# One bias product per half of an expert's hidden row, with a selector kept in memory

## The chip, the cores and the metric

The kernel runs on one core of a Trainium2 chip. A core has TensorE (PE; its weight loads are listed as PEld), VectorE (DVE), ScalarE (ACT), GpSimd (POOL), a sync engine (SP) that issues most transfers here, and 16 DMA engines that the queues share. The metric is the device time of one launch in microseconds, lower is better. Before the change: 1108.92 us, the median of 3 runs (1108.81 to 1109.72).

## The reference

One decoder layer on 256 positions of width 1024, in float32. Its first half (an mLSTM group and an attention group of heads, then an output projection) ends in a residual stream x. Then comes the part that the change touches, a mixture of experts:

```python
logits = (t @ w_router + b_router)            # t: 256 x 1024, the normed stream
top_vals, top_idx = lax.top_k(logits, TOP_K)  # 4 of 32 experts
for e in range(N_EXPERTS):                    # 32
    hu = t @ w_gu[e] + b_gu[e]                # 1024 -> 2048
    glu = jnp.minimum(hu[:, :D_FF], SWIGLU_LIMIT)
    lin = jnp.clip(hu[:, D_FF:], -SWIGLU_LIMIT, SWIGLU_LIMIT)
    act = glu * jax.nn.sigmoid(SWIGLU_ALPHA * glu) * (lin + 1.0)
    y = y + gates[:, e:e + 1] * (act @ w_dn[e] + b_dn[e])
```

After it a gate product of 1024 x 1024 with a per-layer embedding is added. An expert's weights are 12 MB, those of all experts 403 MB, and each byte is read once.

## The kernel before

**Experts.** Each expert works on up to 64 positions (SLOTS), its own, gathered out of the 256 by a product with a one-hot matrix. If some expert has more, the whole expert loop is run again over the rest; in the profiled run it goes through once. Experts are taken in pairs, 16 of them (PAIRS). The gathered rows of a pair lie transposed in `xg` (in `xg0` for the first pair): 8 blocks of 128 input rows, 128 columns, 64 for each expert of the pair.

**The hidden row.** `hu` is PSUM, 4 banks of 128 partitions x 512. Expert e of a pair uses banks 2e (the gate half, b = 0) and 2e + 1 (the linear half, b = 1). The 1024 columns of each half are folded: columns 0 to 511 (n = 0) go to partitions 0 to 63, columns 512 to 1023 (n = 1) to partitions 64 to 127. A product `mm(out, weights, moving)` loads `weights` (rows x output partitions) and streams `moving` (rows x 512) through them. Each float32 product shows as two records in the profile. `up_block` (line 1091) does this for one block of 128 input rows: four products of 64 output partitions each, for b and n. `up_chunk` (line 1137) takes one 2 MB piece of weights, two such blocks; an expert has four of these, then two 2 MB pieces for `down_chunk` (line 1158).

**The bias.** `bias` (line 126) is a tile of 128 rows x 1024. Rows 0 to 31 hold columns 0 to 1023 of `b_gate_up` for the 32 experts, rows 32 to 63 hold columns 1024 to 2047, rows 64 to 95 hold `b_down`. Two DMAs of 128 KB fill the first two (lines 488 and 489), behind SP's wait for `gate_step` and before the loads of `negbc` and `w_out`. `up_bias` (line 1084) adds an expert's row to `hu` by four products, for b and n: the weights are one column of an identity (`sel_part`, rows 32b to 32b + 31), repeated 64 times by a stride of zero, so that every output partition receives the row of that expert.

**Order on PE.** The order is written out by hand. In a pair: the chunks of expert 0 with the scatter of the pair before in between; the first chunk of expert 1; the transposes of expert 0's activation (`act_transposes`, line 1100); the bias of expert 1 (line 1211); expert 0's down products; the rest of expert 1; the gather for the next pair (`gather_half`, line 1039, one-hot products); transposes of expert 1; the bias of the next pair's expert 0 (line 1253); expert 1's down products. The bias of the very first expert stands behind its third chunk (line 1156). Down products wait for ACT's copy of the transposed activation (line 2001).

**The ring of weights.** Eleven slots of 2 MB. SP issues the loads in order of use (`load_position`, line 496; line 514 is nearly every one of them), each when PE has finished with the slot's previous content (`chunk_done`). The last two loads into it are those of the final gate product (line 599).

**DVE and ACT in the loop.** `activation(e)` (line 1668) on DVE takes the minimum and clip of `hu`, ACT's `sigmoid` (line 1995) writes into the same bank, DVE multiplies. Then PE transposes and ACT copies (`transposed_act`, line 1999).

**Memory that the change uses.** `num_xg` holds early things and then, in the loop, expert output (columns 0 to 511), the one-hot matrix (512 to 767), and `gatesT` on partitions 64 to 95 of columns 768 to 1023. Partitions 0 to 63 of these columns are free in the loop. `ident` is a 128 x 128 identity.

Of the kernel before, what the change touches and what calls it, by code (L numbers as in the profile page):

```python
# [33 lines left out]
def hybrid_layer(nc, x, p, mix_norm_g, w_in, conv_w, conv_b, igate_b, fgate_b, mlstm_head_g, q_norm_g,  # L34
# [66 lines left out]
    with ctx:  # L101
# [94 lines left out]

        xg = num_xg[:, VX:VX + K * P].rearrange("p (k s) -> p k s", k=K)
        onehot = num_xg[:, NB:NB + S].rearrange("p (t e s) -> p t e s", t=TT, e=2)
        gatesT = num_xg[64:64 + E, NB + S:NB + 2 * S]
        ghot = early[:, 0:2 * S].rearrange("p (t e r s) -> p t e r s", t=TT, e=2, r=2)  # L200
        ghotT = early[:, 2 * S:4 * S].rearrange("p (e t) -> p e t", e=2)
# [127 lines left out]
        ghotT_ready = sem("ghotT_ready")  # L329
        xg_ps = sem("xg_ps")  # L330
        xg_ready = sem("xg_ready")
        glu_ready = sem("glu_ready")
        lin_ready = sem("lin_ready")
        sig_ready = sem("sig_ready")
# [14 lines left out]
        w_pp_k = w_ple_proj[0].rearrange("(k p) n -> p k n", p=P)  # L349
        gu_src = w_gate_up[0].rearrange("e (p c k) n -> e c p (k n)", c=4, k=2)  # L350
        dn_src = w_down[0].rearrange("e (h p f) n -> e h p (f n)", h=2, f=4)
        x_src = x[0].rearrange("(t p) d -> p t d", p=P)
        p_src = p[0, 0].rearrange("(t p) d -> p t d", p=P)
        out_dst = out[0].rearrange("(t p) d -> p t d", p=P)
# [106 lines left out]
        def _(sp):  # L461
# [23 lines left out]
            load(CHUNK_WO_B, slot(CHUNK_WO_B, D, 4), w_out_k[:, 4:8, :])  # L485
            sp.wait_ge(gate_step, GATE_STEPS)
            sp.dma_start(w_r[:], w_router[0].rearrange("(k p) e -> p k e", p=P)).then_inc(wr_loaded, 16)
            for j in range(2):
                sp.dma_start(bias[32 * j:32 * j + E, :], b_gate_up[0][:, j * D:(j + 1) * D]).then_inc(late_loaded, 16)
            sp.dma_start(bias[64:64 + E, :], b_down[0]).then_inc(late_loaded, 16)  # L490
            sp.wait_ge(negm_stored, 16)
            sp.dma_start(negbc.rearrange("p h s -> p (h s)"), negm_d.rearrange("h s -> (h s)").rearrange("(o n) -> o n", o=1)
# [202 lines left out]
        def _(pe):  # L695
# [381 lines left out]
                              start=(k == 0), stop=(k == PLE // P - 1))  # L1077
                last.then_inc(ple_ps, 1)

            def expert_rows(part, expert):  # L1080

                return sel_part[32 * part:32 * part + E, expert:expert + 1].to_broadcast([E, SLOTS])

            def up_bias(e, expert, first):

                for b in range(2):
                    for n in range(HALVES):
                        mm(hu[n * SLOTS:(n + 1) * SLOTS, 2 * e + b, :], expert_rows(b, expert),  # L1088
                           bias[32 * b:32 * b + E, n * NB:(n + 1) * NB], start=first, stop=False, skip_group_check=True)

            def up_block(e, rows_of, w, k, first, halves=range(2)):

# [39 lines left out]
            with pe.Fori(0, npass) as ps:  # L1132
                for pair in range(PAIRS):
# [3 lines left out]
                    def up_chunk(e, c):  # L1137
                        m = position(pair, 0, e, c)
                        if m in HALVED:
                            wait_half(pe, ps, m)  # L1140
                        wait_position(pe, ps, m)
                        if m == RING + 1:
                            pe.wait_ge(next_half, ps * 16 + 16)
                        w = moe_slot(m)
                        rows_of = xg if pair else xg0
                        first = c == 0 and (e == 1 or pair == 0)
                        if m == 0:
                            for b in range(2):
                                up_block(e, rows_of, w, 0, first, [b]).then_inc(half_done, 1)
                        else:  # L1150
                            last = up_block(e, rows_of, w, 2 * c, first)
                        if m == 1:
                            last.then_inc(half_done, 1)
                        up_block(e, rows_of, w, 2 * c + 1, False).then_inc(chunk_done, 1)
                        if c == 2 and e == 0 and pair == 0:
                            up_bias(0, 0, False)

                    def down_chunk(e, h, bank):
# [49 lines left out]
                        pe.wait_ge(ghotT_ready, pairs + (pair + 1))  # L1208
                    pe.wait_ge(act_ready, experts + (2 * pair + 1))
                    act_transposes(2 * pair)  # L1210
                    up_bias(1, 2 * pair + 1, False)
                    if pair == 0:
                        pe.wait_ge(gates_ready, TT)
                        gate_rows()
                    if pair < PAIRS - 1:
                        if pair == PLE_PAIR:
                            wait_position(pe, ps, PLE_AT)
                            pe.wait_ge(y_done, ps * (QUADS * ROUNDS) + (pair * QUADS + QUADS))
                            embedding_transposes()
                        pe.wait_ge(actT_ready, experts + (2 * pair + 1))  # L1220
                        down_chunk(0, 0, po[:, 0, :])
                        if pair == PLE_PAIR:
                            pe.wait_ge(pT_ready, ps + 1)
                            ple_quad(0)
                        down_chunk(0, 1, po[:, 0, :])
                        if pair == PLE_PAIR:
                            ple_quad(1)
                        if pair == NEXT_PAIR:
                            pe.wait_ge(onehot_ready, pairs + (selections(pair) + 1))
                            pe.wait_ge(y_done, ps * (QUADS * ROUNDS) + (pair * QUADS + QUADS))  # L1230
                            for c in range(2):
                                gather_half(c, aux[:, c, :])
                        up_chunk(1, 1)
                        if pair == PLE_PAIR:
                            ple_quad(2)
                        up_chunk(1, 2)
                        if pair == PLE_PAIR:
                            ple_quad(3)
                        up_chunk(1, 3)

                        pe.wait_ge(onehot_ready, pairs + (selections(pair) + 2))
                        if pair == PLE_PAIR:
                            pe.wait_ge(ple_ready, ps * QUADS + QUADS)
                        elif pair == NEXT_PAIR:
                            pe.wait_ge(xg_ready, ps * (2 * PAIRS) + (gathers(pair) + 2))
                        elif pair == 0:
                            pe.wait_ge(gatesT_ready, ps + 1)
                        pe.wait_ge(y_done, ps * (QUADS * ROUNDS) + (pair * QUADS + QUADS))
                        for c in range(2):
                            gather_half(c, aux[:, c, :])  # L1250
                        pe.wait_ge(act_ready, experts + (2 * pair + 2))
                        act_transposes(2 * pair + 1)
                        up_bias(0, 2 * pair + 2, True)
                        pe.wait_ge(out_s_ready, experts + (2 * pair + 1))
                        pe.wait_ge(actT_ready, experts + (2 * pair + 2))
                        for h in range(2):
                            down_chunk(1, h, po[:, 0, :])
                        if pair == 0:
                            pe.wait_ge(ghot_ready, pairs + 1)
                            ghot_transposes()  # L1260
                    else:
                        for c in range(1, 4):
                            up_chunk(1, c)
                        pe.wait_ge(actT_ready, experts + (2 * pair + 1))
                        down_chunk(0, 0, po[:, 0, :])
                        pe.wait_ge(act_ready, experts + (2 * pair + 2))
                        act_transposes(2 * pair + 1)
                        down_chunk(0, 1, po[:, 0, :])
                        pe.wait_ge(actT_ready, experts + (2 * pair + 2))
                        w = moe_slot(POSITIONS - 2)  # L1270
                        pe.wait_ge(down_half, ps * 16 + 16)
                        down_rows(2 * pair + 1, 0, w, hu[:, 0, :], range(0, 2))
                        pe.wait_ge(out_s_ready, experts + (2 * pair + 1))
                        pe.wait_ge(y_done, ps * (QUADS * ROUNDS) + (pair * QUADS + QUADS))
                        for q in range(HALVES):
                            scatter_expert(q, 0, LAST_BANKS[q])
                        wait_position(pe, ps, POSITIONS - 2)
                        down_rows(2 * pair + 1, 0, w, hu[:, 0, :], range(2, 4)).then_inc(chunk_done, 1)
                        down_chunk(1, 1, hu[:, 0, :])
# [489 lines left out]
        def _(act):  # L1769
# [214 lines left out]
            for tt in range(TT):  # L1984
                act.wait_ge(negtop_ready, tt + 1)
                a.activation(gates[:, tt, :], lg[:, tt, :], ACT.Exp, bias=stat[:, 32 + tt:33 + tt]).then_inc(route_exp, 1)

            act.wait_ge(npass_ready, 1)
            npass = act.value_load(npass_i[0:1, 0:1], min_val=1, max_val=S // SLOTS)
            with act.Fori(0, npass) as ps:  # L1990
                for pair in range(PAIRS):
# [3 lines left out]
                    def sigmoid(e):  # L1995
                        act.wait_ge(glu_ready, experts + (2 * pair + e + 1))
                        a.activation(hu[:, 2 * e, :], gated(2 * pair + e), ACT.Sigmoid, scale=ALPHA).then_inc(sig_ready, 1)  # L1997

                    def transposed_act(e):
                        act.wait_ge(actT_ps, experts + (2 * pair + e + 1))  # L2000
# [92 lines left out]
```

## Time and profile before

| what | value |
|---|---|
| median of 3 runs | 1108.92 us |
| profiled execution | 1109.2 us |
| its span | 1107.0 us |
| granted clock of TensorE, mean | 0.998 of full speed |
| PE busy | 1069.9 us, 97% of the span |
| DVE, ACT, POOL busy | 258.4, 144.7, 17.3 us |
| moved by DMA | 431.89 MB, 390 GB/s over the span |
| bias products (line 1088) | 256 records, 34.8 us busy |

The span is the time from the first to the last instruction that the profile has; some microseconds lie around it. Busy time of PE counts the records' union, in which each record is a few tenths of a microsecond longer than the step to the next one, since matmuls are pipelined. How long a group really occupies PE is read from the starts of the pieces in the chain of waits, where the next piece begins when the last is through.

### The profile page before, as it was taken

To read this page: it belongs to the slowest core of one execution; us is meant where nothing else is said; L and a number is where in the kernel's file an instruction comes from. 1 tells how busy PE (TensorE), PEld (TensorE's weight loads), DVE (VectorE), ACT (ScalarE), POOL (GpSimd) and SP (SyncE) were. 2 spreads that over 40 slices of the span, in tenths; PEclk is the share of its full clock that TensorE was granted. 3 is DMA by queue.
4 is the path that set the end of the run, shared out by engine and by line. 5 is a ranking of instruction groups with operands and counts; after the bars stand their busy time and mean duration, and the time that the engine had idled before them with its cause. 6 is when DMAs were issued, how large, how long until landed. Compare 5 with 4: busy or idle time off the path is not lost.

```text
span 1107.0 us, 12035 instructions
## 1 busy us (share of the span) xinstructions
PE 1069.9 (97%) x5130; PEld 445.0 (40%) x5130; DVE 258.4 (23%) x531; ACT 144.7 (13%) x283; POOL 17.3 (2%) x45
## 2 busy tenths in 40 slices
PE   9999999999999999999999899998989999999898
PEld 5485563434343434343434232333333344433234
DVE  4274241231121212121212121111212021212122
ACT  4134341100000000000000000000000100000022
POOL 2001100000000000000000000000000000000000
PEclk9999999999999999999999999999999999999999
DMA  9943589999999999999999999999999999999981
GB/s 348 368 163 123 242 350 384 427 428 427 427 427 429 427 427 426 429 428 427 427 429 429 427 426 429 429 428 426 427 428 426 427 428 428 427 428 427 425 342 38
DMA packets 43004, 431.89 MB, mean 390 GB/s; under 512 B 6231, under 2 KB 6751, under 8 KB 17606
## 3 DMA queue, kind: packets, MB, share of 16 engines
q1 hardware_dynamic: 42736, 431.07, 93.1%
q8 instruction: 41, 0.67, 0.2%
q14 instruction: 13, 0.11, 0.0%
q10 hardware_dynamic: 214, 0.04, 0.0%
HBM read 430.04 MB, written 1.06 MB: 389 GB/s over the span
## 4 chain that ended last, share of the span: by engine, by line
PE 69%; DMA 30%; DVE 0%; issue 0%; ACT 0%; ACTq 0%; DVEq 0%
PE hu L1096 23%; DMA ring<-in_w_gate_up 22%; PE po L1126 15%; DMA ring<-in_w_down 8%; PE aux L1043 5%; PE hu L723 5%; PE hu L729 3%; PE aux L1051 3%; PE hu L739 2%; PE hu L1088 2%; PE hu L765 1%; PE aux L1303 1%; PE po L1103 1%; PE aux L1076 1%; PE hu L1126 1%; PE po L1303 1%
## 5 line engine op out<-in xcount | busy, mean ns | idle before, releaser
L1096 PE MATMUL hu<-ring,num_xg 128*64 128x512 f32 x1920 | 431.6, 596 | 24.1 <-DMA ring<-in_w_gate_up 24.1
L1096 PEld LDWEIGHTS hu<-ring,num_xg 128*64 128x64 f32 x1920 | 131.5, 137 | 304.2 <-issue 257.2
L1126 PE MATMUL po<-ring,arena 128*64 128x512 f32 x976 | 219.3, 600 | 7.2 <-DMA ring<-in_w_down 7.2
L1126 PEld LDWEIGHTS po<-ring,arena 128*64 128x64 f32 x976 | 67.9, 137 | 154.3 <-issue 139.9
L1674 DVE TENSOR_SCALAR arena<-hu 128x512 f32<-128x512 f32 x31 | 21.4, 692 | 432.0 <-PE hu L1096 432.0
L1650 DVE TENSOR_TENSOR arena<-arena,aux 128x512 f32<-128x512 f32 x58 | 37.3, 684 | 133.3 <-PE aux L1051 121.4
L1043 PEld LDWEIGHTS aux<-num_xg,big 128*128 128x128 f32 x512 | 58.4, 192 | 13.0 <-issue 13.0
L1043 PE MATMUL aux<-num_xg,big 128*128 128x128 f32 x512 | 61.4, 278 | 0.0
L723 PE MATMUL hu<-ring 128*128 128x512 f32 x128 | 56.7, 595 | 0.0
L1997 ACT ACTIVATE hu<-arena 128x512 f32<-128x512 f32 x31 | 18.6, 601 | 249.0 <-DVE arena L1674 249.0
L1663 DVE TENSOR_SCALAR arena<-iota_s,posm,gates 128x128 f32<-128x128 f32 x64 | 17.9, 342 | 118.2 <-PE po L1126 115.3
L2013 ACT COPY arena<-po 128x512 f32<-128x512 f32 x16 | 9.4, 586 | 220.6 <-PE po L1116 220.6
L1051 PE MATMUL aux<-num_xg,arena 64*128 64x512 f32 x124 | 35.0, 641 | 0.1
L723 PEld LDWEIGHTS hu<-ring 128*128 128x128 f32 x128 | 23.8, 190 | 27.7 <-issue 27.4
L1088 PE MATMUL hu<-bias,sel_part 32*64 32x512 f32 x256 | 34.8, 612 | 0.0
L1051 PE MATMUL aux<-arena 64*128 64x512 f32 x124 | 31.8, 589 | 0.0
L2001 ACT COPY arena<-po 128x512 f32<-128x512 f32 x31 | 18.2, 586 | 90.3 <-PE po L1103 90.3
L729 PE MATMUL hu<-ring 128*128 128x256 f32 x128 | 29.5, 385 | 0.0
L1096 PE MATMUL hu<-ring,arena 128*64 128x512 f32 x128 | 28.1, 594 | 0.1
L729 PEld LDWEIGHTS hu<-ring 128*128 128x128 f32 x128 | 23.7, 190 | 4.8 <-DVE ring L1453 1.0
L739 PE MATMUL hu<-ring 128*128 128x512 f32 (+1 forms) x64 | 25.5, 541 | 0.0
L2005 ACT COPY num_xg<-po 128x512 f32<-128x512 f32 x16 | 9.4, 586 | 114.9 <-PE po L1126 114.9
(275 smaller groups left out, 606.5 us busy)
## 6 DMA issues: line engine op xcount, KB each, us to landing
ring<-in_w_gate_up SPq DMA_DIRECT2D x125, 2048.0 KB, 36.0
ring<-in_w_down SPq DMA_DIRECT2D x60, 2048.0 KB, 36.1
ring<-in_w_in SPq DMA_DIRECT2D x6, 2048.0 KB, 16.2
ring<-in_w_gate_up SPq DMA_DIRECT2D x6, 1024.0 KB, 7.7
ring<-in_w_out SPq DMA_DIRECT2D x2, 2048.0 KB, 12.2
ring<-in_w_down SPq DMA_DIRECT2D x4, 1024.0 KB, 37.6
ring<-in_w_ple_gate SPq DMA_DIRECT2D x2, 2048.0 KB, 34.1
ring<-in_w_in SPq DMA_DIRECT2D x4, 512.0 KB, 6.5
```

Source lines behind the costliest of these rows:

```text
L723: last = mm(bank, hT[:, k, tt * P:(tt + 1) * P], slot(n, NB, K)[:, k, :], start=(k == 0), stop=(k == K - 1))
L729: last = mm(bank[:, 0:S], slot(n, NB, K)[:, k, ct * P:(ct + 1) * P], hT[:, k, :], start=(k == 0), stop=(k == K - 1))
L739: last = mm(bank[:, lo:hi], mixT[:, k, tt * P:(tt + 1) * P], slot(n, D, 4)[:, k % 4, b * NB + lo:b * NB + hi], start=(k == 4), stop=(k == 3))
L1043: last = mm(bank[:, (k % 4) * P:(k % 4 + 1) * P], h2[:, tt, k * P:(k + 1) * P], onehot[:, tt, :, :].rearrange("p e s -> p (e s)"), start=( ...
L1051: return mm(bank, ghotT[r, e, tt * P:(tt + 1) * P], out_s[e][r, :], start=(e == 0), stop=(e == 1 and not more))
L1088: mm(hu[n * SLOTS:(n + 1) * SLOTS, 2 * e + b, :], expert_rows(b, expert), bias[32 * b:32 * b + E, n * NB:(n + 1) * NB], start=first, stop= ...
L1096: last = mm(hu[n * SLOTS:(n + 1) * SLOTS, 2 * e + b, :], rows_of[:, k, e * SLOTS:(e + 1) * SLOTS], w[:, o:o + NB], start=first, stop=(k == ...
L1126: last = mm(bank[n * SLOTS:(n + 1) * SLOTS, :], actT[:, f, h * SLOTS:(h + 1) * SLOTS], w[:, o:o + NB], start=(h == 0 and f == 0), stop=(h ...
L1303: last = mm(fin_bank(q, lo, hi), x3T[:, k, tt * P:(tt + 1) * P], final_slot(k // 4, D, 4)[:, k % 4, n * NB + lo:n * NB + hi], start=(k == ...
L1650: v.tensor_tensor(quad(xt, q), quad(xt, q), banks[q], ALU.add).then_inc(y_done, 1)
L1674: v.tensor_scalar(glu, hu[:, 2 * e, :], LIMIT, None, ALU.min).then_inc(glu_ready, 1)
L1997: a.activation(hu[:, 2 * e, :], gated(2 * pair + e), ACT.Sigmoid, scale=ALPHA).then_inc(sig_ready, 1)
```

## The change

The bias rows are loaded in another layout: rows 32n to 32n + 31 hold column half n, both the gate part and the linear part, 64 rows in all. `up_bias` then needs one product for b instead of two: 64 rows by 128 output columns. Its weights are no longer a repeated column but a real tile, `bias_rows`, of 64 rows x 128: for an expert x, row x is one in the left 64 columns, and row 32 + x is one in the right 64. ACT writes it by one copy for each expert (`selector`), out of `ident` with a repeated column, alternating between two places. The first two are written before the loop, after the first gather, the one for expert x + 2 right behind the sigmoid of expert x. PE waits for a new semaphore, `bias_rows_ready`, before each `up_bias`.

```diff
+        bias_rows = num_xg[0:HALVES * E, NB + S:NB + 2 * S].rearrange("p (i n s) -> p i n s", i=2, n=HALVES)
...
+        bias_src = b_gate_up[0].rearrange("e (b n c) -> n e b c", b=2, n=HALVES)
...
-            for j in range(2):
-                sp.dma_start(bias[32 * j:32 * j + E, :], b_gate_up[0][:, j * D:(j + 1) * D]).then_inc(late_loaded, 16)
+            for n in range(HALVES):
+                sp.dma_start(bias[E * n:E * n + E, :].rearrange("e (b c) -> e b c", b=2), bias_src[n]).then_inc(late_loaded, 16)
...
-            def expert_rows(part, expert):
-
-                return sel_part[32 * part:32 * part + E, expert:expert + 1].to_broadcast([E, SLOTS])
-
             def up_bias(e, expert, first):
 
                 for b in range(2):
-                    for n in range(HALVES):
-                        mm(hu[n * SLOTS:(n + 1) * SLOTS, 2 * e + b, :], expert_rows(b, expert),
-                           bias[32 * b:32 * b + E, n * NB:(n + 1) * NB], start=first, stop=False, skip_group_check=True)
+                    mm(hu[:, 2 * e + b, :], bias_rows[:, expert % 2, :, :].rearrange("p n s -> p (n s)"),
+                       bias[0:HALVES * E, b * NB:(b + 1) * NB], start=first, stop=False, skip_group_check=True)
...
+                            pe.wait_ge(bias_rows_ready, experts + 1)
                             up_bias(0, 0, False)
...
+                    pe.wait_ge(bias_rows_ready, experts + (2 * pair + 2))
                     up_bias(1, 2 * pair + 1, False)
...
+                        pe.wait_ge(bias_rows_ready, experts + (2 * pair + 3))
                         up_bias(0, 2 * pair + 2, True)
...
+            def selector(expert):
+
+                both = ident[0:HALVES * E, 0:HALVES * E].rearrange("p (n e) -> p n e", n=HALVES)
+                a.copy(bias_rows[:, expert % 2, :, :], both[:, :, expert:expert + 1].to_broadcast([HALVES * E, HALVES, SLOTS]))\
+                 .then_inc(bias_rows_ready, 1)
+
+            act.wait_ge(xg_ps, 2)
+            selector(0)
+            selector(1)
...
                         a.activation(hu[:, 2 * e, :], gated(2 * pair + e), ACT.Sigmoid, scale=ALPHA).then_inc(sig_ready, 1)
+                        selector((2 * pair + e + 2) % E)
```

## Rows read from the trace of the kernel before

**Rows 1.** strips by slice, the whole span.
```profile
PE   9999999999999999999999899998989999999898
DMA  9943589999999999999999999999999999999981
GB/s 348 368 163 123 242 350 384 427 428 427 427 427 429 427 427 426 429 428 427 427 429 429 427 426 429 429 428 426 427 428 426 427 428 428 427 428 427 425 342 38
```

**Rows 2.** stretches; at the end of a row clock, DMA share, GB/s.
```profile
120.00:140.00 20.00, 20.00 (x89) 12.01 (x88) 5.46 (x12) 4.21 (x11) 2.31 (x2) 1.00 0.79 326
176.00:200.00 24.00, 24.00 (x121) 7.91 (x118) 2.68 (x4) 2.14 (x4) 0.00 (x0) 1.00 1.01 430
1080.00:1100.00 20.00, 20.00 (x63) 10.92 (x62) 5.83 (x14) 7.17 (x14) 0.00 (x0) 1.00 0.10 40
```

**Rows 3.** groups on PE; busy us, mean ns, idle before, releaser.
```profile
L1096 PE MATMUL hu<-ring,num_xg 128*64 128x512 f32 x1920 | 431.6, 596 | 24.1 <-DMA ring<-in_w_gate_up 24.1
L1126 PE MATMUL po<-ring,arena 128*64 128x512 f32 x976 | 219.3, 600 | 7.2 <-DMA ring<-in_w_down 7.2
L1088 PE MATMUL hu<-bias,sel_part 32*64 32x512 f32 x256 | 34.8, 612 | 0.0
L1060 PE MATMUL aux<-bias,num_xg 32*128 32x512 f32 x8 | 4.0, 613 | 0.0
```

**Rows 4.** chain of waits: start us, us, what, xrecords; four pieces.
```profile
177.72 1.02 PE hu L1088 x8
437.19 1.91 PE aux L1060 x4
511.71 1.02 PE hu L1088 x8
542.37 40.04 DMA ring<-in_w_gate_up
```

**Rows 5.** line 514, all expert weight loads; us from issue to landing.
```profile
DMA to landing us min/median/max: 7.1/36.0/46.7
```

**Rows 6.** line 514, the one load issued at 182.4 us.
```profile
DMA to landing us min/median/max: 11.6/11.6/11.6
```

**Rows 7.** line 514, the one load issued at 233.0 us.
```profile
DMA to landing us min/median/max: 10.2/10.2/10.2
```

**Rows 8.** weight loads of lines 1088 and 1060; ns min/median/max.
```profile
L1088 PEld LDWEIGHTS hu<-bias,sel_part x256: 127/129/131, 177.6 to 1038.7; 32*64 32x64 f32 x128
L1060 PEld LDWEIGHTS aux<-bias,num_xg x8: 181/184/185, 437.1 to 445.5; 32*128 32x128 f32 x8
```

**Rows 9.** timeline of PE, first and last of 28 waits for weights.
```profile
577.55 3.65 PE L1096 MATMUL hu<-ring,num_xg 128*64 128x512 f32 x16 [1.04 <-DMA ring<-in_w_gate_up]
1058.89 3.65 PE L1126 MATMUL po<-ring,arena 128*64 128x512 f32 x16 [0.47 <-DMA ring<-in_w_down]
```

**Rows 10.** PE's waits from 822 us to the end: us, times, longest.
```profile
PE hu L1096 <- DMA ring<-in_w_gate_up: 5.2, 6, 1.2
PE po L1126 <- DMA ring<-in_w_down: 3.4, 3, 1.6
```

**Rows 11.** line 1887, the nearest ACT copy to the selector.
```profile
L1887 ACT COPY num_xg<-aux x8: 268/268/271, 114.7 to 140.0; 128x130 f32<-128x130 f32 x8
```

**Rows 12.** timeline of ACT around one bias group: start us, us.
```profile
508.38 0.60 ACT L1997 ACTIVATE hu<-arena 128x512 f32<-128x512 f32 x1 [3.73 <-DVE arena L1674]
511.75 0.59 ACT L2001 COPY arena<-po 128x512 f32<-128x512 f32 x1 [2.77 <-PE po L1103]
```

**Rows 13.** timeline of SP's queue: start us, us, issue.
```profile
41.72 7.83 SPq L489 DMA_DIRECT2D bias<-in_b_gate_up  x2
53.99 0.39 SPq L468 DMA_DIRECT2D ring<-in_w_out  x1
```

**Rows 14.** last loads (line 599); what held line 1303.
```profile
DMA to landing us min/median/max: 31.9/34.1/36.4
  DMA ring<-in_w_ple_gate: 0.2, 1
```

More of the change, by code:

```diff
@@ L331, in hybrid_layer @@
         xg_ready = sem("xg_ready")
+        bias_rows_ready = sem("bias_rows_ready")
         glu_ready = sem("glu_ready")
```

## The prediction

> **What bounds the kernel now.** I read four views, in this order. First the strips by slice: PE is busy everywhere, but from the eighth slice to the thirty-eighth the DMA strip is at 9 and the rate stands at 425 to 429 GB/s [rows 1]. Two things are full at once, and only one can set the end. Then the table of stretches: the DMA share is 0.79 at 120 to 140 us, 1.01 at 176 to 200 us, and 0.10 at 1080 to 1100 us [rows 2]. So the run has three parts: up to about 176 us PE works through the layer's first half and the DMA engines have gaps; from there to about 1074 us they never stop; after that PE alone works off the last products. Then the groups: in the middle PE idles 24.1 us for gate/up weights and 7.2 us for down weights, 31.3 us in all, and hardly for anything else [rows 3]. That is 31.3 us in which PE had nothing to multiply. Last the chain of waits and the time from issue to landing: the chain runs along PE until 542 us, then crosses to a weight load that took 40 us to land [rows 4]. A 2 MB load that goes out alone lands in 7.1 us; the one issued at 182.4 us took 11.6, the one at 233.0 us 10.2, the median 36.0 and the longest 46.7 [rows 5 to 7]. At about 428 GB/s 2 MB move in 4.9 us, so those 36 us are a queue. PE frees slots faster than the DMA engines refill them, the queue grows, and from 577 us on PE waits for it. The chain follows single releases and so credits PE until 542 us; a load that is issued later behind a queue of several others lands no later. My reading: the expert loop is bound by the weight stream, and PE's work counts only before 176 us, after 1074 us, or where it grows beyond its own waits.
>
> **The change part by part.**
> *The products.* Before, an expert's bias costs four products: part b of two, column half n of two. Each is two records, 8 per expert, 256 in all. The four use different rows (0 to 31, 32 to 63) and different output columns (0 to 63, 64 to 127), and the trace shows them side by side: 8 records pass in 1.02 us of the chain [rows 4], 0.13 us per record, where line 1060 needs 0.48. After the change there are two products on the same 64 rows, each over all 128 output columns, so the second can't run beside the first. The trace has no 64-row one of this kind alone, but line 1060 is near: 32 rows, 128 columns, two products on the same rows. Its 4 records take 1.91 us [rows 4]. I read this as a first weight load that shows, 0.18 us [rows 8], and 4 records of (1.91 - 0.18) / 4 = 0.43 us. The old group has the same form: 0.13 us [rows 8] and two steps of 0.43 us are 0.99 of its 1.02. So the new group costs 1.91 us, and the old one 1.02: 0.89 us more for each expert, over 32 experts 28.5 us more of PE. Halving the number of products makes the work longer. If the weight load is hidden, it is 1.72 us, 0.70 more, 22.4 in all. If each of the 4 records shows its own weight load, it is 4 x (0.43 + 0.18) = 2.44 us, 1.42 more, 45.4 in all. Should a product of this kind cost no more than half of the present group, PE would save 0.51 us per expert, the bound on the other side. I take 0.89, by line 1060.
>
> The Trainium skill, "TensorEngine Tiling (Array Packing)", Theoretical Speedup, says that products with at most 64 contraction rows and at most 64 output columns can share the array, up to twice in each direction. It speaks against this change: the old form used the sharing in both directions (the trace agrees: 8 records in 1.02 us), the new one gives both up. By that rule taken strictly, with an array shared four ways, the old group would be 0.86 us and the new one 1.72; that is 0.86 more and 27.5 in all, and the end comes out as with my value.
>
> *What hides it.* PE's waits for weights are the cover: 31.3 us against 28.5 [rows 3]. The order matters, since a lag can only be paid off by a later wait. The first wait is at 577.55 us, the last at 1058.89 [rows 9], 28 in number. Walking through them with 0.89 added at each bias group: PE is 14.2 us behind at 577 us (16 groups), pays this back in the waits up to 820 us, is on time at 820 us, is up to 2.6 us behind in the heavier pairs 12 to 15, and on time again at 1054 us. From 822 us on there are 8.6 us of waits [rows 10] and 8 groups at 0.89, 7.1 us, so 1.5 us remain. Net at the end: 0. The price at which this cover is gone is 31.3 / 32 = 0.98 us per expert.
>
> *What is late next.* A lag of PE also frees slots later. That costs only where the DMA queue is short. The shortest is the load issued at 233.0 us, with 10.2 us to landing [rows 7]; three bias groups come before it, 2.7 us, which leaves 7.5 against 7.1 for a lone load [rows 5]. The one at 182.4 us has 11.6 and one group ahead of it: 10.7 left [rows 6]. So at 233 us the stream is just unbroken; with a start a little slower it would lose 0.1 to 0.3 us. I put down +0.1 us. Later the queue outgrows the lag: near 577 us it is some 46 us long against 14.2.
>
> *The selector on ACT.* 34 copies of 64 x 128. The nearest row is a 128 x 130 copy, 0.27 us [rows 11]; bounds 0.1 and 0.6 (a 512-wide one, [rows 12]). In the loop it stands between the sigmoid, which ends at 508.98 us, and the copy that starts at 511.75 us when PE has transposed [rows 12]: 2.7 us free, 0.27 used, and 2.1 still free if it were 0.6. Behind it on ACT only that copy waits, and DVE's release by the sigmoid stands before it. The first two selectors run after the first gather, near 168 us; PE wants the first at 177.72 [rows 4], and ACT's next work, the first sigmoid, comes after the chunk behind that. Cost 0.
>
> *PE's added waits.* The selector for an expert is written one whole expert earlier, so the wait is met when it is reached. Behind it are the down products of the previous expert. Nothing on PE stands still; a passed wait already sits before the transposes and shows no gap. Cost 0, and if each took 0.1 us, the price per expert would be 0.99, on the threshold.
>
> *The bias loads.* The same 256 KB in pieces of 2 KB instead of 4 KB. SP is occupied by them for 7.83 us from 41.72 us; then it has two small issues, the last done at 50.5 us, and its next work is at 53.99 us, when PE frees a slot [rows 13]. Free in between: 3.5 us. If the issue took twice as long, the w_out load would go out 4.3 us later, at 58 us, but PE reads it after 135 us; the gate/up load at 71.6 us waits for PE anyway. Cost 0.
>
> *The tail.* The last gate product starts when the first of its two loads lands: its weight load waited 0.2 us for it [rows 14]. From there PE works alone for 28 us. No bias is in there.
>
> **Sum.** Span 1107.0 + 0.1 = 1107.1; the profiled execution took 1109.2, 2.2 more than its span, so it would take 1109.3. The median of the runs is 1108.92, 0.3 under the profiled one. I forecast 1109.1 us: no change that can be measured.
>
> **The rivals.**
> *PE becomes the bound (slower).* One mechanism: the new group costs over 0.98 us more than the old one, because weight loads show inside it. If two of its four records show theirs: 1.72 + 2 x 0.18 = 2.08, 1.06 more, 33.9 in all, less 31.3: +2.6, 1111.7 us. If all four do: 45.4 - 31.3 = +14.1, 1123.3 us. For it: the cover left is only 2.8 us over the whole loop. Against it: line 1060 has the same pattern on the same rows and shows one load, not four. Its sign would be that no PE wait for weights is left. Chance 0.16.
> *The chain is right (slower).* If PE's stretch up to 542 us counts as the chain has it [rows 4], the 15 groups in it add 13.3 us: 1122.4. Against it: a DMA share of 1.01 from 176 us, and landing times that only grow. Chance 0.03.
> *The merged product is cheaper.* At half of the old group PE saves 16 us, and all of it turns into more waiting for weights: 1108.9 us. The time is the same as in my forecast. Chance 0.06.
> *Something in the stream gets faster,* for instance because fewer loads are queued. The rate is 430 GB/s at 176 to 200 us with a short queue [rows 2] and mostly 427 or 428 later; if the whole loop ran at 430, 0.5% of some 900 us, 4.5 us, 1104.8. Against it: it is 425 to 429 in every later slice, whether loads take 12 or 46 us. Chance 0.07.
> *The cover holds, nothing moves,* my forecast: 0.68.
>
> **How the numbers follow.** A difference of 0.2%, 2.2 us, is about what can be told from none here. Same: forecast 0.68 and cheaper product 0.06, less 0.02 for spread: 0.72. Slower: 0.16 and 0.03, plus 0.01: 0.20. Faster: 0.08 with spread. The range goes down to 1106.8, which leaves 0.07 below it, and up to 1113.5, which takes in the case of two shown weight loads and leaves about 0.1 for the larger ones.
>
> **What would show it.** The bias group should have 128 records on PE, and pieces of 1.9 us in place of 1.02 (wrong if under 1.1 or over 2.1). PE's waits for weights should shrink from 31.3 us to about 3 and begin near 815 us rather than 577; the DMA strip should stay full and its rate 428 GB/s; landing times should be shorter in the middle (about 32 us at 577 us rather than 46) and as before at the end. The forecast is wrong if no PE wait remains before the last down products, or if the DMA share has a hole near 235 us of more than some tenths.

## The result, and the profile after

The changed kernel takes 1111.37 us (median of 22 runs, 1110.62 to 1113.79), the kernel before in the same session 1109.34 us (22 runs, 1108.06 to 1111.52): a ratio of 1.0019, 95% interval [1.0013, 1.0025]. It is slower by 2.0 us. That is just inside the 0.2% that the forecast called no change, but the interval leaves out 1: with this many runs it is a real loss, and small as it is, its cause can be pointed at. The profiled execution took 1111.1 us, its span is 1108.9.

The strips of the changed kernel, busy tenths and GB/s:

```profile
PE   9999999999999999999999999998989999999998
DMA  9943589999999999999999999999999999999981
GB/s 349 365 163 126 244 350 389 414 393 428 428 427 428 428 426 428 428 427 427 428 428 427 427 428 427 427 428 427 428 427 426 426 430 428 426 428 427 426 352 39
```

The DMA strip reads as before, 9 after 9, and hides the loss. The rate shows it: the eighth and ninth slices, 194 to 249 us, have 414 and 393 GB/s where [rows 1] have 427 and 428. The table of stretches finds the holes. A row has the length of the stretch, the busy time of PE, PEld, DVE, ACT and POOL with their records, and at its end TensorE's clock, the DMA share and GB/s:

```profile
176.00:200.00 24.00, 24.00 (x104) 8.26 (x102) 2.67 (x4) 2.35 (x5) 0.00 (x0) 1.00 1.01 429
214.00:244.00 30.00, 29.93 (x139) 10.26 (x136) 12.17 (x21) 2.69 (x6) 0.00 (x0) 1.00 0.97 384
220.00:222.00 2.00, 2.00 (x12) 0.90 (x12) 1.13 (x5) 1.16 (x2) 0.00 (x0) 1.00 0.79 246
226.00:228.00 2.00, 2.00 (x10) 0.63 (x10) 1.54 (x3) 0.00 (x0) 0.00 (x0) 1.00 0.93 287
232.00:234.00 2.00, 2.00 (x10) 0.67 (x12) 1.91 (x3) 0.00 (x0) 0.00 (x0) 1.00 0.89 254
```

The kernel before has, for the same 30 us:

```profile
214.00:244.00 30.00, 29.93 (x144) 10.22 (x142) 12.18 (x21) 2.95 (x5) 0.00 (x0) 1.00 1.01 428
```

30 us at 384 instead of 428 GB/s are 30 x 44 / 428 = 3.1 us of stream that did not flow. At 200 us nothing is missing yet, and from 260 us on nothing more is lost. The same two long stretches, first of the kernel before, then of the changed one:

```profile
176.00:260.00 84.00, 83.93 (x421) 30.92 (x417) 19.22 (x32) 6.86 (x12) 0.00 (x0) 1.00 1.01 429
260.00:1060.00 800.00, 768.72 (x3804) 288.83 (x3805) 154.04 (x276) 61.40 (x104) 0.00 (x0) 1.00 1.01 427
```

```profile
176.00:260.00 84.00, 83.93 (x388) 31.14 (x386) 18.81 (x31) 7.49 (x15) 0.00 (x0) 1.00 1.00 413
260.00:1060.00 800.00, 790.60 (x3703) 303.17 (x3700) 154.37 (x276) 67.00 (x132) 0.00 (x0) 1.00 1.01 427
```

The groups on PE in the changed kernel (busy us, mean ns, idle before), and the weight loads of the new bias products (ns min/median/max):

```profile
L1094 PE MATMUL hu<-ring,num_xg 128*64 128x512 f32 x1920 | 429.4, 595 | 8.2 <-DMA ring<-in_w_gate_up 8.2
L1124 PE MATMUL po<-ring,arena 128*64 128x512 f32 x976 | 216.7, 595 | 1.7 <-DMA ring<-in_w_down 1.7
L1086 PE MATMUL hu<-bias,num_xg 64*128 64x512 f32 x128 | 63.4, 615 | 0.0
L1086 PEld LDWEIGHTS hu<-bias,num_xg x128: 182/187/187, 177.6 to 1042.5; 64*128 64x128 f32 x128
```

The chain of waits (start us, us, what; three pieces), answering to [rows 4]:

```profile
177.68 1.91 PE hu L1086 x4
523.27 1.91 PE hu L1086 x4
721.16 41.81 DMA ring<-in_w_gate_up
```

Half the records, and 1.91 us for a group in place of 1.02. PE's waits for weights fell from 31.3 us to 9.9, and the chain stays on PE until 721 us instead of 542. The first and the last wait that are left:

```profile
753.24 3.65 PE L1094 MATMUL hu<-ring,num_xg 128*64 128x512 f32 x16 [0.47 <-DMA ring<-in_w_gate_up]
1060.79 3.65 PE L1124 MATMUL po<-ring,arena 128*64 128x512 f32 x16 [0.47 <-DMA ring<-in_w_down]
```

The last one answers to the second of [rows 9]: the same product started at 1058.89 before and at 1060.79 now, both times when its weights landed. PE is on time; the weights are 1.9 us late. Behind it nothing differs.

On ACT the selector (the COPY with `num_xg<-ident`) takes 0.28 us and ends 2.6 us before the copy that it could delay:

```profile
519.93 0.60 ACT L2007 ACTIVATE hu<-arena 128x512 f32<-128x512 f32 x1 [3.73 <-DVE arena L1675]
520.47 0.28 ACT L1992 COPY num_xg<-ident 64x128 f32<-64x128 f32 x1
523.31 0.58 ACT L2012 COPY arena<-po 128x512 f32<-128x512 f32 x1 [2.56 <-PE po L1101]
```

### The profile page after: what moved, and what is told of

Read it like the earlier page. It is cut to its first block, busy times and chain, and to the rows that moved or that the text cites. A ratio compares the mean times of both kernels' runs of the same rounds, so it can differ in the third digit from the quotient of the medians.

```text
span 1108.9 us, 11814 instructions
## 1 busy us (share of the span) xinstructions
PE 1093.1 (99%) x5002; PEld 460.1 (41%) x5002; DVE 258.3 (23%) x531; ACT 151.9 (14%) x317; POOL 17.3 (2%) x45
## 4 chain that ended last, share of the span: by engine, by line
PE 84%; DMA 15%; DVE 0%; issue 0%; ACT 0%; ACTq 0%; DVEq 0%
PE hu L1094 32%; PE po L1124 17%; DMA ring<-in_w_gate_up 11%; PE aux L1046 5%; PE hu L726 5%; PE hu L1086 5%; PE aux L1054 4%; DMA ring<-in_w_down 3%; PE hu L732 3%; PE hu L742 2%; PE po L1101 1%; PE hu L768 1%; PE aux L1304 1%; PE aux L1079 1%; PE po L1114 1%; PE hu L1124 1%
## 5 line engine op out<-in xcount | busy, mean ns | idle before, releaser
L1124 PE MATMUL po<-ring,arena 128*64 128x512 f32 x976 | 216.7, 595 | 1.7 <-DMA ring<-in_w_down 1.7
L1675 DVE TENSOR_SCALAR arena<-hu 128x512 f32<-128x512 f32 x31 | 21.4, 691 | 421.7 <-PE hu L1094 421.7
L1086 PE MATMUL hu<-bias,num_xg 64*128 64x512 f32 x128 | 63.4, 615 | 0.0
L2024 ACT COPY arena<-po 128x512 f32<-128x512 f32 x16 | 9.4, 585 | 220.5 <-PE po L1114 220.5
L726 PEld LDWEIGHTS hu<-ring 128*128 128x128 f32 x128 | 23.8, 190 | 27.7 <-issue 27.4
L1086 PEld LDWEIGHTS hu<-bias,num_xg 64*128 64x128 f32 x128 | 21.4, 186 | 20.1 <-issue 16.3
L2012 ACT COPY arena<-po 128x512 f32<-128x512 f32 x31 | 18.1, 585 | 81.4 <-PE po L1101 81.4
L2016 ACT COPY arena<-po 128x512 f32<-128x512 f32 x15 | 8.8, 585 | 125.3 <-PE po L1124 125.3
## 6 DMA issues: line engine op xcount, KB each, us to landing
ring<-in_w_down SPq DMA_DIRECT2D x60, 2048.0 KB, 32.5
```

The lines of the kernel that those rows point to most:

```text
L726: last = mm(bank, hT[:, k, tt * P:(tt + 1) * P], slot(n, NB, K)[:, k, :], start=(k == 0), stop=(k == K - 1))
L1086: mm(hu[:, 2 * e + b, :], bias_rows[:, expert % 2, :, :].rearrange("p n s -> p (n s)"), bias[0:HALVES * E, b * NB:(b + 1) * NB], start=fir ...
L1124: last = mm(bank[n * SLOTS:(n + 1) * SLOTS, :], actT[:, f, h * SLOTS:(h + 1) * SLOTS], w[:, o:o + NB], start=(h == 0 and f == 0), stop=(h ...
L1675: v.tensor_scalar(glu, hu[:, 2 * e, :], LIMIT, None, ALU.min).then_inc(glu_ready, 1)
L2016: a.copy(out_s[e], bank).then_inc(out_s_ready, 1)
```

## The experiments

Nine kernels, each timed beside the kernel before; a time is the median of 11 runs, but of 5 in E6 and of 4 in E7. They are numbered E1 to E9, in the order in which they ran. In seven of them a small extra product stands behind chosen bias groups of the kernel before, or bias products are left out, so that only PE's time at one place moves.

**E1, selectors and waits alone.**

ACT writes `bias_rows`, and PE waits for `bias_rows_ready` at its three places, as in the change. The bias loads and the four products of `up_bias` are those of the kernel before.

> The kernel before with only the selector side of the change: ACT writes the 34 selectors and PE waits for them ahead of each bias group, but the four old products stay. Theory Q (the queue of loads runs short): the changed kernel is slower by about 2 us because its first three bias groups put PE 2.7 us behind by 212 us, when only about 10 us of loads are queued; the weight stream breaks three times between 220 and 242 us and loses 2.9 us there for good. The selectors have no part in it: ratio to before 1.000, PE's waits for weights 31 us, no hole in the stream. Rival S (the selectors and waits cost it): ratio 1.002, with ACT's copies of the transposed activation later and PE idle before the down products.

1109.23 us, ratio 0.9999 [0.9990, 1.0008]; 427 GB/s at 214 to 244 us. The selector side costs nothing that can be seen, and rival S falls.

**E2, an extra product in the first three groups only.**

```diff
+            def filler(expert):
+                if expert < 3:
+                    mm(po[0:SLOTS, 0, :], sel_part[0:E, 0:1].to_broadcast([E, SLOTS]), bias[0:E, 0:NB], start=True, stop=True,
+                       skip_group_check=True)
...
                             up_bias(0, 0, False)
+                            filler(0)
...
                     up_bias(1, 2 * pair + 1, False)
+                    filler(2 * pair + 1)
...
                         pe.wait_ge(out_s_ready, experts + (2 * pair + 1))
+                        filler(2 * pair + 2)
```

> The kernel before with one extra product (32 rows, 64 columns, into a bank that is cleared afterwards) behind the bias groups of experts 0, 1 and 2 only: 0.86 us each, 2.6 us in all, by the row of line 1060 without its weight load. Theory Q: all of the loss is there: ratio 1.002, the loads issued at 217 to 240 us go out 2.6 us later and by 250 us the landings are 2.5 to 3 us late; PE's waits for weights stay near 31 us, since nothing else grew. Rival T (the total: 28.5 us of added PE work nearly uses up 31.3 us of waits and some of it comes through): 2.6 of 28.5 us added, a tenth of the loss, ratio 1.0002.

1111.56 us, ratio 1.0020 [1.0011, 1.0030]. Its chain (the old group, then the extra product) and its stretch:

```profile
211.15 1.02 PE hu L1095 x8
212.16 0.84 PE po L1088 x2
```

```profile
214.00:244.00 30.00, 29.93 (x142) 10.09 (x140) 12.19 (x21) 2.70 (x5) 0.00 (x0) 1.00 0.98 385
```

Three times 0.84 us, 2.5 us of PE work in all, bring the whole loss of the change, with the same drop to 385 GB/s. PE's waits for weights are 32.5 us, as many as before.

**E3, the extra product in the other 29 groups** (`if expert >= 3`).

> The kernel before with that extra product behind the bias groups of experts 3 to 31, 29 times 0.86 = 24.9 us of added PE work, the first three groups untouched. Theory Q: none of it is seen: ratio 1.000, PE's waits fall from 31.3 to about 6 us, landings up to 250 us as before. Rival T: most of the loss, ratio 1.0017.

1109.40 us, ratio 0.9999 [0.9990, 1.0008], with 24.4 us (29 x 0.84) more PE work. Its waits for gate/up weights shrank:

```profile
PE hu L1103 <- DMA ring<-in_w_gate_up: 10.0, 8, 1.8
```

With the 1.8 us for down weights 11.8 us are left of 31.3, not 6; the part on the cover below says why. This is ten times the added work of E2 and none of its loss: rival T falls.

**E4, the changed kernel with the first three groups cut.**

```diff
-                for b in range(2):
+                for b in range(1 if expert < 3 else 2):
                     mm(hu[:, 2 * e + b, :], bias_rows[:, expert % 2, :, :].rearrange("p n s -> p (n s)"),
```

The linear half of these three experts gets no bias. For expert 2, whose bias product was the first to write its bank, the first weight product now starts the bank.

> The changed kernel with the second bias product (linear half) left out for experts 0, 1 and 2, so that their groups take 0.18 + 0.86 = 1.04 us instead of 1.91, like the old ones; experts 3 to 31 as changed. The output lacks these three biases. Theory Q: back to the time of before: ratio to before 1.000, no hole at 220 to 242 us, PE's waits about 31.3 - 25.8 = 5.5 us. Rival T: nine tenths of the loss stay, ratio 1.0018. Rival L (the new layout of the bias loads, or anything else in the first half): ratio stays 1.002 too, and then landings are late before 217 us.

1108.96 us, ratio 0.9999 [0.9990, 1.0008]. One product with its weight load takes 1.05 us, about the old group's time; expert 3 has the merged group of 1.91 us:

```profile
209.51 1.05 PE hu L1086 x2
241.17 1.91 PE hu L1086 x4
```

The merged product in 29 of 32 experts, the selectors and the new layout are all still in it, and the loss is gone. Rivals T and L fall too. The rate at 214 to 244 us is 413 GB/s here. That is no net loss against the kernel before: this execution's landings are 1.1 us ahead of it at 204 us (202.5 against 203.6 us, for the load issued at 191.6 us in both), and by 277 us the two are 0.2 us apart.

**E5 and E6, how much a delay at that place costs.** One extra product behind expert 0 only, and two behind each of the first three.

> The kernel before with the extra product (0.84 us, measured in the run with three of them) behind the bias group of expert 0 only. PE is 0.84 us late where the load of 233 us goes out: the load before it lands at 238.2, so it goes out 4.4 us ahead of that, against 5.2 before and 2.6 to 2.8 in the slow kernels. Theory Q1 (the stream stays whole as long as a load goes out some 4 us or more before the last one lands): ratio 1.000 to 1.0005. Theory Q2 (every delay at this place is paid in full): 0.84 us, ratio 1.0008.

> The kernel before with two extra products behind each of the first three bias groups: PE 5.1 us late at 213 us. Theory Q: holes in every gap between 217 and 242 us; loads then take about 8.5 to 9.3 us to land as in the changed kernel, the one issued at 237.2 + 5.1 lands at about 251.6 instead of 248.1, so the landings are 3.5 to 6 us late from there on, ratio 1.003 to 1.005. Rival H (the loss is a fixed thing, one break in the stream, whatever its length): as with one extra product each, ratio 1.002.

The first: 1109.64 us, ratio 1.0005 [0.9996, 1.0014], too small to tell Q1 from Q2 by the time. The second: 1113.46 us, ratio 1.0040 [1.0026, 1.0054], so rival H falls. The landing of one and the same load, in the profiled executions, says more. It is issued at 259.6 us in the kernel before and lands 17.8 us later, at 277.4. In the others it is issued at 260.4 (E5, one extra product), 262.0 (E2, three), 263.1 (the change) and 265.1 (E6, six), and takes, in this order,

```profile
DMA to landing us min/median/max: 17.8/17.8/17.8
```

```profile
DMA to landing us min/median/max: 18.8/18.8/18.8
```

```profile
DMA to landing us min/median/max: 17.2/17.2/17.2
```

and 18.3 us. So it lands 0.8, 3.4, 2.9 and 6.0 us late, for delays of PE of 0.84, 2.5, 2.7 and 5.1 us in the first three groups. (In the change the issue itself is 3.5 us late, since a fourth bias group stands before it.) The landings are not exact to better than some tenths: of the 6.0 us of E6 0.4 were there before the first bias group (the load of 71.6 us goes out at 72.0), and E1 and E3, which have no delay there, land this load 0.4 and 0.3 us early. Within that, it is for Q2: by 277 us a delay at this place is paid about in full. The medians of the whole time grow by less, 0.5, 2.1, 2.0 and 4.3 us; why is not settled, and more is said below.

**E7, more PE work than PE has waits,** with two extra products in each of the 29 groups.

> The kernel before with two extra products behind the bias groups of experts 3 to 31: 29 x 1.69 = 49 us of added PE work, more than the 31.3 us of waits. It tests the other bound, the cover. By the sum of the prediction, added work less waits: +17.7 us, ratio 1.016, and no PE wait for weights is left. If PE's waits were no real cover (the stream itself being slowed by PE's work), one extra product each would have shown it already.

1119.77 us, ratio 1.0094 [1.0079, 1.0110]; the profiled span is 1117.7. No wait of PE for expert weights is left:

```profile
L1103 PE MATMUL hu<-ring,num_xg 128*64 128x512 f32 x1920 | 427.6, 595 | 0.0
L1133 PE MATMUL po<-ring,arena 128*64 128x512 f32 x976 | 216.6, 595 | 0.0
```

Two extra products take 1.70 us:

```profile
242.68 1.70 PE po L1088 x4
```

The bound has changed sides as forecast, but the price is 10.7 us and not 17.7: of 29 x 1.70 = 49.3 us added, 38.6 were covered. The column of idle time holds only 31.3.

**E8, the new layout with the four old products.**

```diff
-                        mm(hu[n * SLOTS:(n + 1) * SLOTS, 2 * e + b, :], expert_rows(b, expert),
-                           bias[32 * b:32 * b + E, n * NB:(n + 1) * NB], start=first, stop=False, skip_group_check=True)
+                        mm(hu[n * SLOTS:(n + 1) * SLOTS, 2 * e + b, :], expert_rows(n, expert),
+                           bias[E * n:E * n + E, b * NB:(b + 1) * NB], start=first, stop=False, skip_group_check=True)
```

> The new bias layout (rows 0 to 31 column half 0, rows 32 to 63 column half 1, loads in 2 KB pieces) with the old four products of 32 rows x 64 columns, each on the rows of its column half, no selector. Now only two of the four products have array parts of their own; the two of one column half use the same rows and the same columns. Theory P (products overlap only where both rows and columns differ): 0.13 + 4 x 0.43 = 1.85 us per group, like the merged product, ratio 1.002. Rival P2 (the saving in the old form came from narrow products as such, or from PSUM banks): 1.02 us per group and ratio 1.000. It also tells whether the merging or the layout lost the overlap.

1111.44 us, ratio 1.0018 [1.0009, 1.0028], and in the chain

```profile
522.79 1.86 PE hu L1089 x8
```

The same 8 records of the same shape take 1.86 us instead of 1.02. So rival P2 falls, and the loss of overlap comes with the layout: the two products of one column half now need the same rows and the same columns. Merging them into 128 columns on top of that added only 0.05 us. The wording of theory P was too strict, though. The gate/up products of the kernel share all 128 rows and differ in columns alone, and 16 of their records pass in 3.43 us of the chain, 0.21 each, half of the 0.43 that a record alone takes. Different columns are enough; in E8 neither rows nor columns differ within a half. The row, of three times 16 records in the kernel before:

```profile
195.02 10.30 PE hu L1096 x48
```

**E9, PE earlier instead of later.** The kernel before without any bias product for experts 0 to 2 (`for b in range(0 if expert < 3 else 2)`; expert 2's banks are then started by its first weight products).

> The kernel before without any bias products for experts 0, 1 and 2 (their gate/up biases are missing in the output): PE is 1.02 us earlier per group, 3.1 us by 212 us. In the trace of before the stream at 214 to 244 us is whole (428 GB/s), yet delays of 0.84, 2.6 and 5.1 us there made the landings at 260 us late by 0.8, 3.4 and 5.9, nearly their own size. Theory Q (the stream is full and can't go faster; only holes cost): landings at 260 us as before, ratio 1.000. Rival E (PE still paces the stream at that place, so an earlier PE gains what a later one loses): landings about 3 us earlier and ratio 0.997, and then shorter PE work there would beat both kernels.

1109.31 us, ratio 0.9996 [0.9987, 1.0005]: no gain, rival E falls, and an earlier PE at the sensitive place does not beat the kernel before. Its profile is of little use for landings, since that execution (1111.19 us, the slowest of its eleven) was 1.9 us late already at the load of the output weights (issued at 40.8 us against 38.9). It does show that cutting a bias group is not all gain: PE then waited for ACT's copy, which the group had covered. So PE gained some 2 us by 217 us, not the 3.1 expected: the load of 217.7 us goes out at 217.6, in an execution that had been 1.9 us late. At 2 us, rival E would still have given 0.998, which the interval leaves out.

```profile
186.49 0.69 PE po L1103 x4
187.21 0.59 ACT arena L2001
187.84 7.09 PE po L1126 x32
```

## Why the prediction was right, and where it was not

**The price of the group: right to the hundredth.** 1.91 us by line 1060, 1.91 measured. The way it was put together also holds: E4's group of two records takes 1.05 us and the full one of four 1.91, so two records are 0.86, 0.43 each, and 0.19 is left, the length of one weight load. Halving the number of products made the work longer by 28.5 us.

**What bounds the loop: right.** 24.4 us of added PE work in 29 groups left the time alone (E3), so did 25.8 us in the merged form (E4). PE's chain up to 542 us did not count, and the rival that took it at its word is out.

**The selector, the waits, the bias loads: right.** E1 shows it for the first two, in which the time stays. SP is held 8.04 us by the bias loads instead of 7.83 and issues the load of the output weights at 53.95 us instead of 53.99. The rival of a faster stream found nothing to live on: the rate from 260 to 1060 us is 427 GB/s in both kernels.

**What is late next: the place about right, the size wrong.** This is the step that failed: "which leaves 7.5 against 7.1 for a lone load", and from it +0.1 us. The prediction named the load of 233.0 us, and PE was late there by 2.6 us, about as named. But the one of 217.7 us, behind the same three groups, has hardly more room and was not looked at:

```profile
DMA to landing us min/median/max: 10.8/10.8/10.8
```

The rate fell from 220 us on, in three holes. And the comparison with the lone load was no measure of when the stream breaks. In the changed kernel these two loads, issued at 220.3 and 235.6 us, took 8.5 and 8.9 us:

```profile
DMA to landing us min/median/max: 8.5/8.5/8.5
```

```profile
DMA to landing us min/median/max: 8.9/8.9/8.9
```

They were issued 3.3 and 3.9 us before the load ahead of them landed, and still the rate fell to 246 GB/s at 220 us. In the kernel before the tightest of them was issued 5.2 us ahead, with no hole. A lone load takes 7.1 us, of which 4.9 are transfer at the full rate, and I had taken a lead of the other 2.2 us to be enough. What the runs show in its place is that, for these 2 MB loads, a lead of 5.2 us keeps the stream whole and leads of 3.3 to 3.9 us do not; E5, with leads of 4.2 to 5.5 us, lost 0.8 us. The rows above tell one part of it: at 220 to 222 us the DMA share is 0.79 although the load ahead lands only at 223.6 us. This reads as some of the 16 engines having run out while others still worked at that load; a landing would then tell only when the last of them is through. Why the lead must be as long as it is, no run here tells. The loss by 260 us is 2.9 us by landings and 3.1 by the rate. The prediction had named a sign for this, a hole in the DMA share near 235 us, and that sign came: 0.89 at 232 to 234 us, and 0.79 at 220 to 222.

**Why 2.0 us at the end and not 2.9.** Set side by side, load by load, the landings of the two profiled executions differ by 2.9 us from 250 us on, but by 1.3 between 420 and 450 us, 2.9 again later, 1.3 near 870 and 2.0 near 1050. Now and then a load lands 1.0 to 1.7 us later than the step of 4.9 us from the load before it would have it: in the kernel before at 391, 598, 815 and 1029 us, in the changed kernel at 458, 675 and 904 us. The stream itself makes no such pause. Here are the stretches before the first two of these landings in the kernel before, and before the second in the changed kernel:

```profile
386.00:391.00 5.00, 5.00 (x24) 1.59 (x22) 1.28 (x2) 0.00 (x0) 0.00 (x0) 1.00 1.02 429
592.00:598.00 6.00, 6.00 (x30) 1.87 (x26) 0.00 (x0) 0.00 (x0) 0.00 (x0) 1.00 1.02 431
```

```profile
669.00:675.00 6.00, 6.00 (x28) 1.96 (x28) 1.28 (x2) 0.00 (x0) 0.00 (x0) 1.00 0.98 415
```

Even 415 GB/s for 6 us leaves out only 0.2 us of transfer, not 1.5. It is the landings that slip, not the flow. PE's last wait ends with a landing, so the loss that the end shows depends on where these slips fall: 1.9 us in the two profiled executions, 2.0 by the medians, with an interval of 1.4 to 2.8. What makes the landings slip stays open.

**The cover: right in sign, too small.** The prediction had 31.3 us of waits and so a threshold of 0.98 us a group, and expected about 3 us of waits to be left. 9.9 were. A stop seems to hide more than its listed idle time: a block of 16 records takes 3.43 us of PE when the next follows at once, but 3.65 (start to modelled end) when PE waits behind it, as the rows of the waits show. That is 0.22 us for each of 28 stops, 6.2 us in all, and 31.3 + 6.2 = 37.5 us of cover, against 38.6 measured with E7. The threshold can then be estimated at 38.6 / 32 = 1.2 us per group; the rival in which PE becomes the bound was further off than I gave it. For E3 the sum nearly closes: 19.5 us of idle gone, 18 stops fewer (4.0 us) and a last wait 0.3 us later make 23.8 of the 24.4 added. For the changed kernel 21.4 us of idle gone, 17 stops fewer (3.7 us) and a last wait 1.9 us later make 27.0 of the 28.5 added; 1.5 us are not accounted for. PE's waits began at 753 us, where the prediction had 815.

**The forecast as a whole.** The likeliest case, with the cover holding, is what happened, and it was not without a price; the time is 2.3 us over the 1109.1 forecast, in the range. That it lies in the range is partly luck. The upper end of 1113.5 was set for weight loads that show inside the group, and those did not come; the loss from the stream, which did, stood in the sum at 0.1 us. Some sums of the prediction are off by a tenth or two: 1109.3 less 0.3 is 1109.0, and from 1109.1 the rivals come to 1123.2 and 1104.6 us. Nothing hangs on that.

## What to carry to other kernels

Fewer, wider products are not cheaper if the narrow ones ran side by side in parts of the array of their own. Count the steps that remain when products on shared rows and columns follow one another, not the instructions. Added work on an engine that is not the bound is free only where the queue of the bounding resource is long. Look for the place where the time from issue to landing is shortest, here early in the loop, and ask by how much a load's issue runs ahead of the previous landing. A busy strip of tenths can't show such a loss: read the GB/s row and set it against the same stretch before. The landing of one and the same load in both traces helps, but single landings slipped here by up to 1.7 us with the rate unchanged.

## What was not expected of the hardware

- The stream of 2 MB loads broke when loads were issued 3.3 to 3.9 us before the previous one landed, and was whole at 5.2 us; 0.84, 2.5 and 5.1 us of delay of PE there made the landings of 277 us 0.8, 3.4 and 6.0 us late (0.4 of the 6.0 came from earlier).
- A DMA share of 0.93 can go with 287 GB/s (226 to 228 us of the changed kernel), where 1.00 goes with 426 in the kernel before. Packet by packet, its trace shows why the share hides the hole: the packets of 16 KB take 0.61 to 0.62 us there before the change, and after it a quarter of them over 1 us, up to 1.5. An engine counts as busy while its packet is under way.
- PE's idle time before weights understates how much more work could be hidden: 31.3 us listed, 38.6 us usable.
- A load can land 1.0 to 1.7 us behind its step while the rate stays at 415 to 431 GB/s.
